# Attention's first loads and rows of maxima reordered over two queues, values in two halves, and routing's one-hot rows in four parts, in a two-layer diffusion backbone

## The reference, cut to what matters

```python
s = jnp.einsum('bqhgd,bkhd->bhgqk', qblk, k, preferred_element_type=jnp.float32) * scale
p = jax.nn.softmax(s, axis=-1)
return jnp.einsum('bhgqk,bkhd->bqhgd', p.astype(v.dtype), v)
...
counts = jnp.bincount(flat_e, length=N_EXPERTS)
padded = (counts + MOE_BLOCK - 1) // MOE_BLOCK * MOE_BLOCK
dest_sorted = pad_start[sorted_e] + jnp.arange(A) - start[sorted_e]
slot_tok = jnp.zeros((n_blocks * MOE_BLOCK,), jnp.int32).at[dest_sorted].set(order // TOP_K)
block_e = jnp.minimum(jnp.searchsorted(pad_end, jnp.arange(n_blocks) * MOE_BLOCK, side='right'), N_EXPERTS - 1)
xb = h[slot_tok].reshape(n_blocks, MOE_BLOCK, D)
```

## Time and profile before

| | |
|---|---|
| median of 3 runs | 3735.64 us (3735.0 to 3740.15) |
| the profiled execution's own time | 3735.84 us |
| its span, first to last instruction | 3733.7 us |
| granted clock of the matrix engine, mean | 0.944 of 2.4 GHz |
| matrix engine busy (PE) | 3329.1 us, 89% |
| VectorE busy (DVE) | 2712.4 us, 73% |
| ScalarE busy (ACT) | 1851.2 us, 50% |
| GpSimd busy (POOL) | 1447.1 us, 39% |
| DMA queue of POOL (q0) | 528.57 MB, 36.8% of the 16 engines' time |
| DMA queue of SP (q1) | 157.73 MB, 13.8% |
| DMA queue of ScalarE (q10) | 51.92 MB, 3.8% |

### The profile page before, as it was taken

The page is one execution under the profiler, slowest core; times in us unless marked ns, Lnnn a source line. Parts: engine busy times, 40 slices in busy tenths (PEclk is TensorE's granted clock), DMA queues, the critical chain, the costliest instruction groups (busy, mean ns, idle before and its releaser), DMA issues. The chain is left out here.

```text
span 3733.7 us, 44344 instructions
## 1 busy us (share of the span) xinstructions
PE 3329.1 (89%) x14480; PEld 2229.8 (60%) x14480; DVE 2712.4 (73%) x2845; ACT 1851.2 (50%) x2133; POOL 1447.1 (39%) x1089
## 2 busy tenths in 40 slices
PE   6999699999795999999959996999979599999994
PEld 3555355544484788888834444555437488887881
DVE  2444466677586898999866654777768699988996
ACT  1223233344311888888823322333332188888881
POOL 2111011121211777777731110111112287777772
PEclk8999799999896999999979996999999699999997
DMA  7665532211442998698754327221115378997974
GB/s 299 215 228 187 159 95 67 59 48 39 153 150 98 409 364 309 262 361 316 303 219 148 123 89 199 59 64 46 38 45 199 120 288 328 355 362 284 353 287 198
DMA packets 258764, 739.65 MB, mean 198 GB/s; under 512 B 55456, under 2 KB 149440, under 8 KB 205272
## 3 DMA queue, kind: packets, MB, share of 16 engines
q0 software_dynamic: 114288, 528.57, 36.8%
q1 hardware_dynamic: 129816, 157.73, 13.8%
q10 hardware_dynamic: 14544, 51.92, 3.8%
HBM read 723.62 MB, written 129.61 MB: 229 GB/s over the span
## 5 line engine op out<-in xcount | busy, mean ns | idle before, releaser
L2094 DVE TENSOR_TENSOR ex_wl<-ex_wr,ex_wh 128x2048 fp32r<-128x2048 f32 x440 | 988.0, 2286 | 63.0 <-ACT ex_wh L2039 62.8
L2039 ACT ACTIVATE ex_wh<-ex_wr 128x2048 fp32r<-128x2048 f32 x440 | 843.3, 1916 | 76.4 <-PE ex_yp L2002 38.5
L1235 ACT ACTIVATE at_pt<-at_st 128x1024 f32<-128x1024 f32 (+1 forms) x336 | 336.5, 1003 | 546.4 <-PE at_st L1170 545.3
L1281 DVE TENSOR_REDUCE at_nm<-at_sc 128x1 f32<-128x1280 f32 (+1 forms) x276 | 378.4, 1371 | 208.0 <-PE at_sc L1135 205.2
L794 PE MATMUL zp<-w_in,hT 128*128 128x480 f32 x960 | 424.4, 576 | 13.3 <-DMA w_in<-in_w_in 10.3
L1295 DVE TENSOR_TENSOR at_acc<-at_acc,at_pt 128x1024 f32<-128x1024 f32 x256 | 321.0, 1254 | 97.1 <-ACT at_pt L1235 94.5
L1921 POOL DMA_INDIRECT ex_wr<-in_w_down,piece_of x152 | 313.1, 2060 | 46.3 <-issue 46.3
L1184 PE MATMUL at_op<-at_pt,at_va 128*64 128x512 f32 (+1 forms) x1344 | 314.8, 597 | 0.2
L1170 PE MATMUL at_st<-at_q,at_km 96*128 96x512 f32 (+3 forms) x1008 | 266.2, 404 | 16.5 <-DMA at_q<-at_nmT 14.5
L794 PEld LDWEIGHTS zp<-w_in,hT 128*128 128x128 f32 x960 | 172.4, 193 | 162.0 <-issue 139.3
L1914 POOL DMA_INDIRECT ex_xb<-h_s,row_from x76 | 198.6, 2613 | 118.7 <-DVE ex_xb L2097 96.2
(11 more groups left out here) (283 smaller groups left out, 5955.7 us busy)
## 6 DMA issues: line engine op xcount, KB each, us to landing
ad_w<-in_w_ada POOLq DMA_DIRECT2D x48, 1024.0 KB
q_mla<-qT SPq DMA_DIRECT2D x40, 384.0 KB, 3.9
k_mla<-kT SPq DMA_DIRECT2D x40, 384.0 KB, 5.7
at_km<-k_mla SPq DMA_DIRECT2D x16, 960.0 KB
at_q<-q_mla SPq DMA_DIRECT2D x32, 384.0 KB, 21.8
w_in<-in_w_in SPq DMA_DIRECT2D x6, 1920.0 KB, 25.9
q_gqa<-gqT SPq DMA_DIRECT2D x20, 512.0 KB, 6.7
cy<-y_s POOLq DMA_DIRECT2D x10, 1024.0 KB
```

What stands on the lines that cost most here:

```text
L1235: nc.scalar.activation(pt[:, j % PT, :, 0:nq], st[:, j % 2, :, 0:nq], ACT.Exp).then_inc(exp_done, 1)
L1281: nc.vector.tensor_reduce(nm[:, v % 3, s:s + 1], score_bank(A_NO[v, s])[:, 0:kb * P], AX.X, ALU.max, negate=True).then_inc(max_done, 1)
L2039: nc.scalar.activation(wh[:, q], wr[:, u, p], ACT.Copy).then_inc(hi_done, 1)
L2094: nc.vector.tensor_tensor(wl[:, q], wr[:, u, p], wh[:, q].bitcast(F32), ALU.subtract).then_inc(lo_done, 1)
```

## The change

In `attention`, SP loads the coarse queries of all early units, then the coarse keys of the first pair, and waits until these keys are in. Only then does it issue the coarse queries of the second latent unit, the fine keys and the fine queries of the early units. Of each early unit's rows of maxima SP copies the first half, and ScalarE copies the second half on its own queue, right behind `take_row`. The other loads of units 1 and 2 that the prologue doesn't need move behind these rows. POOL no longer waits for loads, but for all rows of the early units, and loads the values as two halves of five tiles with a semaphore each; the matrix engine waits for the second half at key tile 5 of the first latent unit.

In `routing`, the one-hot rows are made in four parts (two choices by two halves of the tiles), each with a comparison for `in_step`, one for `at_slot` and the product with the row number, and the matrix engine waits for each part by itself.

```diff
--- before.py
+++ after.py
@@ -1020,7 +1020,7 @@
         st = cx.enter_context(nc.psum_tensor(f"at_st{layer}", [P, 2, 2, 512], F32))
         sc = cx.enter_context(nc.psum_tensor(f"at_sc{layer}", [P, 1536], F32))
         op = cx.enter_context(nc.psum_tensor(f"at_op{layer}", [P, 512], F32))
-        k_loaded, g_loaded, v_loaded = [[sem(f"k_loaded{s}{x}") for x in range(2)] for s in range(2)], [sem(f"g_loaded{x}") for x in range(2)], sem("v_loaded")
+        k_loaded, g_loaded, v_loaded = [[sem(f"k_loaded{s}{x}") for x in range(2)] for s in range(2)], [sem(f"g_loaded{x}") for x in range(2)], [sem(f"v_loaded{n}") for n in range(2)]
         q_loaded, row_set = [[sem(f"q_loaded{s}{x}") for x in range(2)] for s in range(QR)], [sem(f"row_set{s}") for s in range(QR)]
         ones_set, s_full, exp_done = sem("ones_set"), sem("s_full"), sem("exp_done")
         a_full, max_done, nm_full, nm_out = sem("a_full"), sem("max_done"), sem("nm_full"), sem("nm_out")
@@ -1058,11 +1058,11 @@
 
         @block.sync
         def _(sp):
-            def set_row(v):
+            def set_row(v, half=None):
                 pair, t0, na, kb, nq = place(v)
                 at, x = (QK, 0) if pair < G0 else (HD, 1)
                 sp.wait_ge(nm_out, T_NO[v] + 1)
-                for n in range(2 * na):
+                for n in range(2 * na) if half is None else range(half * na, (half + 1) * na):
                     sp.dma_start(q[at:at + 1, v % QR, x, n // 2, n % 2, :].bitcast(F32),
                                  nmT[n:n + 1, T_NO[v] % 2, :].bitcast(F32)).then_inc(row_set[v % QR], 16)
 
@@ -1071,15 +1071,21 @@
                 sp.wait_ge(ot_ready, u + 1)
                 sp.dma_start(S["o_s"][t0:t0 + na, :, pair, :].rearrange("a p n -> p a n"), ot[:, u % 2, 0:na, :]).then_inc(o_stored[u % 2], 16)
 
-            load_q(sp, 0, 0)
+            for v in early:
+                load_q(sp, v, 0)
             load_k(sp, 0, 0)
-            for u in (1, 2):
-                load_q(sp, u, 0)
+            sp.wait_ge(k_loaded[0][0], 16)
+            load_q(sp, LATENT[1], 0)
             load_k(sp, 0, 1)
-            for u in range(3):
-                load_q(sp, u, 1)
             for v in early:
-                set_row(v)
+                load_q(sp, v, 1)
+            for v in early:
+                set_row(v, 0)
+            for v in range(3):
+                if v not in early:
+                    if v != LATENT[1]:
+                        load_q(sp, v, 0)
+                    load_q(sp, v, 1)
             for x in range(2):
                 load_k(sp, 1, x)
             for x in range(2):
@@ -1175,7 +1181,9 @@
                 pair, t0, na, kb, nq = place(u)
                 j = AT[u] + k
                 if j == 0:
-                    pe.wait_ge(v_loaded, 16)
+                    pe.wait_ge(v_loaded[0], 16)
+                if u == LATENT[0] and k == NT // 2:
+                    pe.wait_ge(v_loaded[1], 16)
                 if k == 0 and u > 0:
                     pe.wait_ge(den_taken, u)
                 pe.wait_ge(exp_done, j + 1)
@@ -1262,6 +1270,11 @@
                                  ones[HD:HD + 1, :].to_broadcast([1, H_KV * NT * P]), ACT.Copy).then_inc(ones_set, 1)
             for v in early:
                 take_row(v)
+                pair, t0, na, kb, nq = place(v)
+                act.wait_ge(nm_out, T_NO[v] + 1)
+                for n in range(na, 2 * na):
+                    act.dma_start(q[QK:QK + 1, v % QR, 0, n // 2, n % 2, :].bitcast(F32),
+                                  nmT[n:n + 1, T_NO[v] % 2, :].bitcast(F32)).then_inc(row_set[v % QR], 16)
             for u in range(len(U)):
                 for k in range(U[u][3]):
                     exponential(u, k)
@@ -1326,9 +1339,11 @@
 
         @block.gpsimd
         def _(pool):
-            pool.wait_ge(k_loaded[0][1], 16)
-            pool.wait_ge(q_loaded[2][1], 16)
-            pool.dma_start(va[:, :, :], S["v_s"].rearrange("(t p) n -> p t n", p=P)).then_inc(v_loaded, 16)
+            for v in early:
+                pool.wait_ge(row_set[v % QR], rows_set(v))
+            for n in range(2):
+                tiles = slice(n * NT // 2, (n + 1) * NT // 2)
+                pool.dma_start(va[:, tiles, :], S["v_s"].rearrange("(t p) n -> p t n", p=P)[:, tiles, :]).then_inc(v_loaded[n], 16)
             pool.dma_start(kg[:, :, :].bitcast(F32), S["k_gqa"][:, 0:H_KV, :]).then_inc(g_loaded[0], 16)
             pool.dma_start(kl[0:HD, :, :].bitcast(F32), S["k_gqa"][0:HD, H_KV:2 * H_KV, :]).then_inc(g_loaded[1], 16)
             for u in range(len(U) - 1):
@@ -1671,6 +1686,7 @@
     nt = NT - t0
     nb = n_blocks(nt)
     MAXB = nt
+    SPLIT = ((0, nt // 2), (nt // 2, nt))
     with ExitStack() as cx:
         new_semaphore = cx.enter_context(semaphores(nc))
 
@@ -1739,9 +1755,11 @@
             nc.tensor.matmul(pp[:, 0:(nt + 1) * NE], C["ones"][:, :], before[:, :, :].rearrange("p t e -> p (t e)"), start=True, stop=False)
             nc.tensor.matmul(pp[:, 0:nt * NE], C["tri"][:, :], cnt[:, :, :].rearrange("p t e -> p (t e)"), start=False, stop=True).then_inc(prefix_done, 1)
 
-            pe.wait_ge(slots_ready, 2)
             for k in range(TOPK):
                 for t in range(nt):
+                    for h, (lo, hi) in enumerate(SPLIT):
+                        if t == lo:
+                            pe.wait_ge(slots_ready, len(SPLIT) * k + h + 2)
                     ins = nc.tensor.matmul(ids[:, 0:nj], at_slot[:, k, t, :], in_step[:, k, t, :],
                                            start=(k == 0 and t == 0), stop=(k == TOPK - 1 and t == nt - 1))
             ins.then_inc(ids_done, 1)
@@ -1825,12 +1843,17 @@
             ch.link(V.scalar_tensor_tensor(first[:, :], T["odd"][:, 0:nj], steps_half[:, 0:1], T["half"][:, 0:nj], ALU.mult, ALU.add))
             ch.link(V.tensor_tensor(again[:, :], T["step_no"][:, 0:nj], filled.to_broadcast([P, nj]), ALU.is_ge))
             ch.link(V.scalar_tensor_tensor(first[:, :], again[:, :], float(FAR), first[:, :], ALU.mult, ALU.add))
-            V.tensor_tensor(at_slot[:, :, :, :], off[:, :, :].unsqueeze(3).to_broadcast([P, TOPK, nt, P]),
-                            T["slot"][:, :].unsqueeze(1).unsqueeze(1).to_broadcast([P, TOPK, nt, P]), ALU.is_equal)
-            ch.link(V.tensor_tensor(in_step[:, :, :, :], dest[:, :, :].unsqueeze(3).to_broadcast([P, TOPK, nt, nj]),
-                                    first[:, :].unsqueeze(1).unsqueeze(1).to_broadcast([P, TOPK, nt, nj]), ALU.is_equal))
-            V.tensor_tensor(in_step[:, :, :, :], in_step[:, :, :, :],
-                            T["row"][:, :, t0:NT].unsqueeze(3).to_broadcast([P, TOPK, nt, nj]), ALU.mult).then_inc(slots_ready, 1)
+            for k in range(TOPK):
+                for lo, hi in SPLIT:
+                    n = hi - lo
+                    part = in_step[:, k, lo:hi, :]
+                    chosen = ch.step(V.tensor_tensor(part, dest[:, k, lo:hi].unsqueeze(2).to_broadcast([P, n, nj]),
+                                                     first[:, :].unsqueeze(1).to_broadcast([P, n, nj]), ALU.is_equal))
+                    V.tensor_tensor(at_slot[:, k, lo:hi, :], off[:, k, lo:hi].unsqueeze(2).to_broadcast([P, n, P]),
+                                    T["slot"][:, :].unsqueeze(1).to_broadcast([P, n, P]), ALU.is_equal)
+                    dve.wait_ge(step, chosen + 1)
+                    V.tensor_tensor(part, part, T["row"][:, k, t0 + lo:t0 + hi].unsqueeze(2).to_broadcast([P, n, nj]),
+                                    ALU.mult).then_inc(slots_ready, 1)
 
             b3 = big[:, 0:NE * nj].rearrange("p (b e) -> p b e", e=NE)
             ch.link(V.tensor_tensor(b3, endb[:, :].unsqueeze(1).to_broadcast([P, nj, NE]),
```

## The result

The changed kernel takes 3744.5 us (median of 20 runs, 3738.93 to 3753.89), the kernel before 3738.49 us (20 runs, 3731.84 to 3746.12) on the same chips: the ratio is 1.0019, 95% interval 1.0013 to 1.0025. The forecast was 3732.8, with a range to 3741. The forecast counted from 3735.84 us; 20 runs of the kernel before have their median 2.65 us above that, so against its own starting point it said -3.0 where +6.0 was measured. The profiled execution has a span of 3745.5 us at a mean granted clock of 0.944, the same clock as before.

What follows compares the result with a forecast made beforehand. The matrix engine, busy 89% of the span, was taken as the bound. Layer 0 +5.3, layer 1 -4.8 and routing -3.5 gave -3.0 us on 3735.84: 3732.8 us, range 3723 to 3741 for 8 in 10.

Steps and rivals of the forecast that it cites:

- No wait, by 0.7 us: Layer 1, first values product: the values' first half lands at 2310.3, before it is wanted at 2311.0.
- its first packets come some 1.5 us after the issue began: Start of POOL's values load behind the rows: a delay of 1.5 us from issue to first packets.
- 0.5 to 1 for values a little late: Allowance for late values in layer 1's bounds, which ran from -6.5 to -2.5 us.
- Layer 1: Attention start there: -4.8 us, from first scores 6.5 earlier and a later wait for rows of +1.7.
- Layer 0: Attention start there: +5.3 us, from a values product 3.8 later and 1.5 for the half clock.
- rows 10 and 11: Profile rows cited for q1's issue order in layer 0: 10 KB packets of keys, then 1 KB packets of queries.
- -6.5 from the rows: Layer 1: rows land before the last maximum, so first scores start at 2301.9 instead of 2308.39.
- holding them back gains nothing: Layer 0 prologue: loads behind the first keys never slowed them, so delaying those loads saves no time.
- The wait for the second unit's rows (+1.7): Layer 1: these rows land at 2338.7 behind q1's queued loads, wanted at 2337.0; +1.7 us, ends 0 and 3.0.
- Routing: End of routing, both layers: matmuls start after each one-hot part, so the sums wait vanishes; -3.5 us (-2.9 to -3.9).
- Values in time: Rival: engines split by time or keys don't hold the values, so layer 0 loses nothing; 3727.5 or 3722 us, chance 0.28.
- Values behind everything: Rival: q0 gets nothing while q1 holds work, +8.2 us in each layer; 3750.5 us in all, chance 0.07.

Runs made afterwards that it cites:

- values_early: Changed kernel, but POOL waits only for the early units' loads, not for their rows, before loading the values; 3730.08 us, ratio 0.9976 to the kernel before.
- no_key_wait: Changed kernel without SP's wait for the first keys; 3744.6 us, ratio 1.0016 to the kernel before.
- keys_held: Changed kernel, but SP issues the loads behind its rows only once the first half of the values is in; 3751.7 us, ratio 1.003 to the kernel before.
- half_early: Changed kernel with unit 0's queries and keys first, values' first half loaded in the prologue, second half and grouped keys behind the rows; 3725.88 us, ratio 0.9967.
- whole_late: Changed kernel with its values in one load behind the rows instead of two halves; 3756.63 us, ratio 1.005 to the kernel before.
- keys_first: Changed kernel with the second early unit's coarse queries issued behind the first keys; 3746.96 us, ratio 1.0019 to the kernel before.

## Why the forecast was wrong

**The step that failed** is the one that ends in "No wait, by 0.7 us", in layer 1, and in it the term "its first packets come some 1.5 us after the issue began". That number came from a queue that started while nothing else moved, and it was used for one that starts beside a busy q1. Measured: over 5 us in layer 1 and close to 6 in layer 0. In those the three query loads of layer 1, small packets beside which the values would have run well, passed nearly alone (1120 packets of q1 from 2308 to 2313, of the 1152 that they make), and the values met nearly all of the keys instead. The same sum with the right start: counted from the first load, the issue is at 2308.12 - 2282.32 = 25.8 and the first packets at about 31.5; 12 packets of values beside keys at 0.87 and 8 beside queries at 0.27 take 12.6, the landing 1.6, and the half is in at 45.7. Measured: 46.53, where the forecast said 2310.3, that is 35.6. The range failed with it, because its low and high ends for layer 1 ("0.5 to 1 for values a little late") had no case in which q0 starts late. Layer 1 alone is 10.1 us off; layer 0 (-0.5) and routing (-0.7) take 1.2 of that back, and 8.9 are left of the 9.0 us between -3.0 and +6.0.

The forecast had a row that hinted at this: the rows of maxima of the kernel before, put into q1 while q0 was flowing, needed 5.4 us where 1.7 is usual. I read it as a price of small packets beside values and not as one that any queue pays which joins a busy one. The traces show the second. In values_early the rows issued at 2298.4 on q1 and on q10, beside a q0 that streams values, have their first packets at 2302.2 to 2302.6 and 2302.6 to 2303.0. In the changed kernel unit 0's rows in layer 0, issued on q10 from 441.20 on beside a busy q1, have none before 446.1. The Trainium skill (DMA: Bandwidth & Descriptors, Latency and other measured facts) gives about 1 us to the first byte of a load from GpSimd. The traces have more: 1.6 us with idle engines and 5 to 6 beside a busy queue.

**Layer 0** was right in size: product at +4.0 for +3.8 forecast, the start of the stage +4.84 for +5.3, an idle of 9.29 us in front of the product within the 5 to 10 named. That was luck in one step, for the queue started 4 to 5 us later than I had it. There the keys went first anyway: a packet of keys that has gone before the values start is one that they don't meet later, so the sum hardly hangs on the start. By 465.8 about 130 of the 192 key packets had gone; four pairs at 0.87, 16 packets at 0.27 and the landing from there give 475.2, and the product stands at 475.14. In layer 1 the sum does hang on it. The first matmul came 1.46 later, for 1.6. (The forecast names rows 10 and 11 the wrong way round for q1's order: the queries of 437 to 439 stand ahead of the keys of 441 to 443. That is their order of issue too, so nothing hangs on it.)

**Layer 1, -4.8 forecast, +5.25 measured.** The first scores are right (-6.5 from the rows, and 0.96 more since the first matmul was earlier). Whether "holding them back gains nothing" is true stays open: no_key_wait is 1.18 us later to its first matmul, but kernels without the wait and with it overlap there. The wait for the second unit's rows (+1.7) didn't come, because the unit before it was late already; with the values in time it is there, 6.47 us in keys_held and 2.60 in half_early.

**Routing, -3.5 forecast (-2.9 to -3.9), -4.2 measured.** The mechanism is right. The operations are what the rows gave: 0.82 us for 640 columns, 0.44 for 270. A part takes 1.44 us for 1.5, and the vector work grew by 0.41 and 0.40 us, where the sum had 0.75 and 0.65.

**The rivals.** "Values in time" is refuted by the packet counts and by the waits of 9.29 and 10.79 us. "Values behind everything" has the right sign and passed its deciding point (a half landing at 2318.5; here it is 2328.85 less the 7.6 us by which the stage started later, 2321.2), but the whole, at +6.0, stayed under its +7.5, and its mechanism is false: q0 is not shut out, it starts late and then alternates. "The change doesn't do what it says" is refuted too: the rows that the scores wait for (layer 1, and unit 1 of layer 0) all land within 2.0 us.

**What stays open.** Why a queue that joins a busy one needs 4 to 6 us to its first packet. It isn't POOL's own, for q1 and q10 show it too (about 4 us in values_early, 5 in the changed kernel). It is much the same beside 1 KB packets (layer 1) and beside 10 KB packets (layer 0), so it isn't the packet in front of it alone. No run here goes further.

## What to carry to other kernels

A wait that keeps a large load away from small urgent ones is paid in idle transfer engines: ask what the load is needed for next, and whether it fits in the window before the small ones, in whole or in the part that is needed first. When two queues share the engines, count packets and not bytes, and price the start of a queue by whether the others are busy then. And after removing a stall look for the next transfer in line: with the first 60 us of a stage short of transfers, much of what was gained before it was taken by the next wait.

## What the hardware showed beyond expectation

- A load of values from POOL beside a busy q1 moved its first packet 5 to 6 us after its issue (459.93, 2308.12, and 2317.84 in whole_late), beside a silent one after 1.6 us (2295.7, and 2310.85 in keys_held). All kernels here agree: twelve such issues beside a busy q1 took 5.0 to 6.4 us, twelve beside a silent one 1.6 to 1.8. The queues of SP and ScalarE start late as well: rows issued at 2298.4 in values_early, beside a busy q0, moved their first packets some 4 us later, and ScalarE's of 441.20 in the changed kernel, beside a busy q1, 5 us later.
- Two queues alternate, about packet for packet, at all sizes seen: in one microsecond 16 packets of 5 KB beside 16 of 10 KB, in another 64 of 5 KB beside 64 of 1 KB.
- The half clock can outlast the wait that it stands behind: in keys_first it held for 10 us of unbroken matmuls, in the changed kernel for some 3.
- A row's DMA of 0.5 KB lands in 1.6 us with silent engines from SP's queue and in 1.7 to 2.0 from ScalarE's; ScalarE needs 2.77 us to issue four, SP 2.48.
